# Three rearrangements in a two-block transformer kernel: modulation insertions joined, the end of a recurrent block taken by chunks, and stick-breaking attention begun inside the stage that makes its values

## The reference, cut to what matters

```python
mod = (s_lat @ w_ada[l] + b_ada[l])[:, None, :]
mod_c = s_ctx @ w_ada[l] + b_ada[l]
...
u = dwconv1d(h @ w_up, dw, dw_b)
a, g = jnp.split(u, 2, axis=-1)
return (jax.nn.silu(g) * a) @ w_down
```

```python
z = jnp.einsum('bhqd,bhkd->bhqk', q[:, :, t0:L], k[:, :, :L])
log_keep = jnp.where(mask, jax.nn.log_sigmoid(-z), 0.0)
later = lax.cumsum(log_keep, axis=3, reverse=True) - log_keep
w = jnp.where(mask, jnp.exp(jax.nn.log_sigmoid(z) + later), 0.0)
outs.append(jnp.einsum('bhqk,bhkd->bhqd', w, v[:, :, :L]))
...
a = jnp.exp(log_a)
b = jnp.sqrt(-jnp.expm1(2.0 * log_a)) * (i * xc).astype(jnp.float32)
_, hs = lax.associative_scan(_lin_rec_combine, (a, b), axis=1)
y = jax.nn.gelu(gate) * hs.astype(h.dtype)
return y @ w_out
```

## Time and profile before

| | |
|---|---|
| median of 3 runs | 2291.49 us (2282.19 to 2295.35) |
| the profiled execution's own time | 2294.72 us |
| its span, first to last instruction | 2293.1 us, mean granted clock 0.989 |
| PE busy | 2210.9 us, 96% |
| DVE busy | 1819.1 us, 79% |
| ACT busy | 1297.8 us, 57% |
| transfers | 499.80 MB, mean 218 GB/s |
| matmuls of three-way products, start to start | 0.12 us |

### The profile page before, as it was taken

One profiled execution on the slowest core, in us unless ns is written; L12 is line 12 of the kernel. 1 busy time (PEld: TensorE's weight loads), 2 busy tenths in 40 slices (PEclk: granted clock), 3 DMA queues, 4 the chain that ended last, 5 costly groups with the idle time before them and its releaser, 6 DMA issues.

```text
span 2293.1 us, 49211 instructions
## 1 busy us (share of the span) xinstructions
PE 2210.9 (96%) x18000; PEld 2122.8 (93%) x18000; DVE 1819.1 (79%) x3186; ACT 1297.8 (57%) x2102; POOL 119.8 (5%) x231
## 2 busy tenths in 40 slices
PE   6999999999999999999999999989999999979998
PEld 4898899998899999889999999987999999979998
DVE  4886867799699988978998878767877877878655
ACT  3465755536776553576665644646544644686443
POOL 0100000000000100000000011010000001000000
PEclk8999999999999999999999999999999999999999
DMA  9746666765358865534778678662778677636654
GB/s 356 277 138 203 230 236 204 257 202 162 123 184 273 271 222 199 176 117 170 256 268 278 225 274 269 213 237 88 247 270 267 236 274 264 235 106 192 219 171 132
DMA packets 150550, 499.80 MB, mean 218 GB/s; under 512 B 17408, under 2 KB 21632, under 8 KB 148864
## 3 DMA queue, kind: packets, MB, share of 16 engines
q1 hardware_dynamic: 113504, 374.01, 47.4%
q0 software_dynamic: 32544, 119.55, 16.5%
q10 hardware_dynamic: 4352, 4.20, 0.6%
HBM read 496.65 MB, written 1.05 MB: 217 GB/s over the span
## 4 chain that ended last, share of the span: by engine, by line
PE 70%; DVE 14%; ACT 6%; DMA 5%; issue 4%; ACTq 0%; DVEq 0%; SPq 0%; POOLq 0%; POOL 0%
PE bank_pair L1922 21%; PE bank_pair L1924 20%; PE bank_pair L1923 20%; DVE w_lo L1173 4%; DMA modraw<-in_w_mod 3%; ACT w_hi L636 2%; DVE arena L1460 2%; PE bank_pair L2045 2%; PE ps_o L1935 1%; DVE small L1540 1%; DVE modraw L1201 1%; ACT arena L875 1%; DVE arena L1329 1%; DMA raw<-in_w_down 1%; PE ps_o L2354 1%
## 5 line engine op out<-in xcount | busy, mean ns | idle before, releaser
L1173 DVE TENSOR_TENSOR w_lo<-raw,w_hi 128x1024 fp32r<-128x1024 f32 (+2 forms) x748 | 821.1, 1113 | 189.1 <-ACT w_hi L636 185.6
L636 ACT ACTIVATE w_hi<-raw 128x1024 fp32r<-128x1024 f32 (+2 forms) x748 | 713.4, 967 | 391.9 <-PE bank_pair L1924 257.6
L1922 PE MATMUL bank_pair<-h_hi,w_hi 128*128 128x256 f32 x2928 | 839.0, 287 | 10.5 <-DVE arena L1737 4.2
L1923 PE MATMUL bank_pair<-h_lo,w_hi 128*128 128x256 f32 x2928 | 829.5, 283 | 0.0
L1924 PE MATMUL bank_pair<-h_hi,w_lo 128*128 128x256 f32 x2928 | 829.4, 283 | 0.0
L1922 PE MATMUL bank_pair<-e_both,w_hi 128*128 128x256 f32 (+1 forms) x2064 | 593.7, 288 | 18.7 <-DVE e_both L1857 10.0
L1922 PEld LDWEIGHTS bank_pair<-h_hi,w_hi 128*128 128x128 f32 x2928 | 561.5, 192 | 31.2 <-issue 24.2
L1923 PE MATMUL bank_pair<-e_both,w_hi 128*128 128x256 f32 (+1 forms) x2064 | 585.6, 284 | 0.0
L1924 PE MATMUL bank_pair<-e_both,w_lo 128*128 128x256 f32 (+1 forms) x2064 | 585.5, 284 | 0.0
L1923 PEld LDWEIGHTS bank_pair<-h_lo,w_hi 128*128 128x128 f32 x2928 | 562.0, 192 | 0.3
L1924 PEld LDWEIGHTS bank_pair<-h_hi,w_lo 128*128 128x128 f32 x2928 | 561.8, 192 | 0.0
(11 more groups left out here) (250 smaller groups left out, 2103.9 us busy)
## 6 DMA issues: line engine op xcount, KB each, us to landing
modraw<-in_w_mod POOLq DMA_DIRECT2D x216, 512.0 KB, 5.0
raw<-in_w_gu SPq DMA_DIRECT2D x176, 512.0 KB, 4.6
raw<-in_w_up SPq DMA_DIRECT2D x132, 512.0 KB, 5.1
raw<-in_w_gate SPq DMA_DIRECT2D x48, 512.0 KB, 3.9
raw<-in_w_dn SPq DMA_DIRECT2D x64, 384.0 KB, 4.6
raw<-in_w_dn SPq DMA_DIRECT2D x64, 320.0 KB, 3.5
raw<-in_w_down SPq DMA_DIRECT2D x48, 384.0 KB, 5.1
raw<-in_w_down SPq DMA_DIRECT2D x48, 320.0 KB, 4.8
```

The lines of the kernel that those rows point to most:

```text
L636: nc.scalar.activation(w_hi[:, p, HALF * f:HALF * f + w], raw[:, p, HALF * f:HALF * f + w], ACT.Copy)\
L1173: nc.vector.tensor_tensor(w_lo[:, p, at], raw[:, p, HALF * f:HALF * f + w], w_hi[:, p, at].bitcast(F32), ALU.subtract).then_inc(lo_ready, 1)
L1922: nc.tensor.matmul(out, l[0], r[0], start=start, stop=False)
L1923: nc.tensor.matmul(out, l[0], r[1], start=False, stop=False)
```

## The change

Three edits in different stages.

1. **Up stage of the context.** Both halves of a modulation and the turn of the one before are now inserted together, between the halves of the slab with p=1 (`whole`). The slab with p=0 has no insertion. The stage's last turn and its sum move from the stage's end into the first slab of the next stage (`last_turn`).
2. **Stick-breaking.** The helpers `st_scores`, `st_terms` and so on replace the inline code. Inside value slab k, between its halves, PE makes scores(k) and, from k=2 on, sums(k-2). DVE has softplus(k-1), mask(k) and add(k-2) there ahead of the modulation products, ACT terms(k-1), and in the last slab weights(0). `do_stick` starts at i=3 (`ST_AHEAD`). Scores go to the banks `ps_t`, sums to `ps_o`, outputs to bank pair 1. The seven unread matmuls are gone. The last two modulation products of the value stage move from iteration 1 to iteration 8. ACT's table load for Exp and Ln stands in the first value slab, before in the last.
3. **End of the recurrence.** The products by the root move ahead of the splits of slab 8, so both stand before the first scan. Low parts 0 to 5 are made before the second scan. In the first body PE takes chunks 0 to 5 of slab 0, chunks 0 to 4 of slab 1, then 6 to 9 of slab 0 and the rest of slab 1, with eight unread matmuls ahead and three between (`LRU_WARM`).

```diff
+        def whole(s):
+            return s.kind == "upa"
...
+        def last_turn(s, b, p):
+            q = s.prev
+            if q is not None and q.turn_end and isinstance(b, int) and (b, p) == (0, 0):
+                return q.m0 + q.mods * q.bodies - 1
+            return None
...
# ACT, value stage
-                        if last and p == 1 and s.arg["heads"] == SB_H:
-                            act.preload_act_table_set("natural_log_exp_and_others")
+                        if s.arg["heads"] == SB_H:
+                            if 2 * b + p == 0:
+                                act.preload_act_table_set("natural_log_exp_and_others")
+                            else:
+                                st_terms(2 * b + p - 1)
+                            if 2 * b + p >= 3:
+                                st_weights(2 * b + p - 3)
...
# DVE, value stage
                         if s.arg["heads"] == SB_H:
-                            lambda_part(4 + 2 * b + p)
+                            k = 2 * b + p
+                            if k >= 1:
+                                st_softplus(k - 1)
+                            st_mask(k)
+                            if k >= 2:
+                                st_add(k - 2)
+                            lambda_part(4 + k)
...
# DVE, do_stick
+                for i in range(ST_AHEAD, SB_P + 3):
+                    if ST_AHEAD < i <= SB_P:
+                        st_softplus(i - 1)
                     if i + 1 < SB_P:
+                        st_mask(i + 1)
+                    st_low(i - 3)
+                    if i <= SB_P:
+                        st_add(i - 1)
+                    if i == SB_P:
                         mods(sv, sv.bodies - 1, 1, False, True)
...
# DVE, recurrence
                         if j == 7:
                             lru_square(1)
+                            for f in range(2):
+                                lru_input(f)
                         if j == 8:
                             lru_scan(0)
...
             def do_lru(n):
                 lru_outs(0)
+                lru_lows(0)
                 lru_scan(1)
-                lru_lows(0)
                 lru_outs(1)
                 lru_lows(1)
...
# PE
             def mods(s, b, p):
-                if s.m0 >= N_PE or not s.mods:
+                if last_turn(s, b, p) is not None:
+                    mod_turns(last_turn(s, b, p))
+                if s.m0 >= N_PE or not s.mods or whole(s) and p == 0:
                     return
...
+            def lout_first(s, p):
+                n, early = RC // 2, LRU_PARTS[0].stop
+                if p == 0:
+                    free_banks(s, 0, 1, True)
+                    pe.wait_ge(lru_gates, RC)
+                    keep_warm(LRU_WARM[0])
+                    pe.wait_ge(lo_ready, 2 * s.l0 + 1)
+                    for k in range(n):
+                        ins = lout_chunk(s, 0, k)
+                    ins.then_inc(half_done, 1)
+                    pe.wait_ge(lo_ready, 2 * s.l0 + 2)
+                    for k in range(n, early):
+                        lout_chunk(s, 0, k)
+                    pe.wait_ge(lo_ready, 2 * s.l0 + 3)
+                    for k in range(n):
+                        lout_chunk(s, 1, k)
+                    keep_warm(LRU_WARM[1])
+                    for k in range(early, RC):
+                        ins = lout_chunk(s, 0, k)
+                    ins.then_inc(half_done, 1)
+                else:
+                    pe.wait_ge(lo_ready, 2 * s.l0 + 4)
+                    lout_chunk(s, 1, n).then_inc(half_done, 1)
+                    for k in range(n + 1, RC):
+                        ins = lout_chunk(s, 1, k)
+                    ins.then_inc(half_done, 1)
...
# PE, value stage
                             half(s, b, p, 0, is_first)
                             mods(s, b, p)
+                            if s.kind == "v" and s.arg["heads"] == SB_H:
+                                st_scores(2 * b + p)
+                                if 2 * b + p >= 2:
+                                    st_sums(2 * b + p - 2)
```

More of the change, by code:

```diff
@@ L1909, in _ @@
                 kinds[s.kind](s) if what == "slabs" else others[what](s)
-                if what == "slabs" and s.turn_end:
-                    mod_sums(s.m0 + s.mods * s.bodies - 1)
         @block.tensor
@@ L2021, in _ @@
                     plain = s["plain"] + DC
+            stick = next(s for what, s in plan if what == "stick")
             def b_is_one(b):
@@ L2197, in out_first, with keep_warm, lout_chunk @@
                             ins.then_inc(half_done, 1)
+            def keep_warm(n):
+                for _ in range(n):
+                    nc.tensor.matmul(ps_t[:, 0, 0:T], ones, table("cos"), start=True, stop=True)
+            def lout_chunk(s, p, k):
+                pe.wait_ge(lru_lo, k + 1)
+                f, n = k // (RC // 2), k % (RC // 2)
+                c = HALF * f + P * n
+                return mm3(pb[p][:, 0, 0:T], (w_hi[:, p, c:c + P], w_lo[:, p, c:c + P]),
+                           (e_hi[:, k, :], e_lo[:, k, :]), k == 0, k == RC - 1)
+            def lout_first(s, p):
[24 more added lines that the diff above has]
+                    ins.then_inc(half_done, 1)
             def open_pair(i):
@@ L2227, in body @@
                             merge_first(s)
+                        elif s is after_lru and is_first:
+                            lout_first(s, p)
                         elif s.kind == "out" and is_first and p == 0:
@@ L2365, in do_gate @@
                     merge_heads(s.nxt, c)
-            def keep_warm(n):
-                for _ in range(n):
-                    nc.tensor.matmul(ps_t[:, 0, 0:T], ones, table("cos"), start=True, stop=True)
             def do_stick(n):
                 so = next(s for what, s in plan if what == "slabs" and s.kind == "out" and s.arg["kind"] == "b")
-                pe.wait_ge(tab_in, 16)
-                pe.wait_ge(q_copied, n["had"]["q"])
-                pe.wait_ge(v_copied, n["had"]["v"] - 1)
-                for i in range(-1, SB_P + 2):
+                pe.wait_ge(v_copied, n["had"]["v"])
@@ L2379, in do_stick @@
+                for i in range(ST_AHEAD, SB_P + 2):
+                    if i == ST_AHEAD:
+                        st_out(0)
                     if i + 1 < SB_P:
[L2380 to L2388 removed]
@@ L2405, in do_stick @@
[L2405 to L2417 removed]
+                        st_scores(i + 1)
```

173 lines of the change are left out of this document (88 added, 85 removed).

## The result

The changed kernel takes 2272.09 us (median of 7 runs, 2270.9 to 2272.97), the kernel before 2291.49 us (7 runs, 2282.19 to 2295.35). The ratio is 0.9923, 95% interval 0.9912 to 0.9934. The profiled execution took 2272.4 us with a span of 2270.7 us; that of before had a span of 2293.1 us. The forecast was 2271 us.

A forecast was written before the change was run, and what follows sets the result against it. PE, busy for 96% of the span, was taken to bound the kernel. Gains of 5.0 + 11.6 + 4.1 = 20.7 us give 2274.0 us from the profiled 2294.72, 2270.8 from the median 2291.49; forecast 2271 us, range 2260 to 2283.

The forecast's parts named there:

- Edit 1, 5.0 us forecast: Up stage: joined insertions save 0.32 us in each of 11 bodies, 3.5 us, and an idle turn's 1.5 us goes.
- so the 1.5 us go: Up stage, second body: the turn, moved behind ACT's copy of its row, no longer stands idle for 1.52 us.
- The last turn only changes place: End of the up stage: the final turn moves without gain or loss, about 0.2 us of matmuls.
- joining saves nothing: Rival, up stage: slabs without insertions end waiting for DVE's taps, gain 0 instead of 5, 2275.8 us; chance 0.08.
- Edit 2, 11.6 us forecast: Value stage and stick-breaking: softplus(3) starts at about 1542.6 instead of 1554.17, then the same 3.9 us a pair.
- The schedule worked out: Value stage and stick-breaking: order laid out by hand from 1505.3, the first value matmul, to softplus(3) at about 1542.6.
- Only one of the six products that I follow waited over 1 us: Value stage: held against the slower case, late loads holding PE up, 2302 us; chance 0.04.
- The reason in one sentence: Stick-breaking before: mask(0) behind four modulation products came 5 us after its scores; the ring filled with nothing else on PE.
- The two products at iteration 8: Stick-breaking: 2.3 us of DVE work makes low part 6 1.1 us later, hidden by PE's output projection; cost nothing.
- The clock: Rival, stick-breaking and recurrence's end: stretches at 1.2 GHz, about 5 us less gain, 2275.8 us; chance 0.10.
- Edit 3, 4.1 us forecast: Recurrence's end: PE through slab 1 4.7 us earlier, less 0.6 us waiting for a bank; bounds 2.5 to 5.
- the fourth slab waits 0.6 us for its bank: Last projection: DVE only 2.6 us earlier with its updates, so PE loses 0.6 us of the 4.7 us gained.

The follow-up runs named there:

- halves_apart: The changed kernel with the two halves of the modulation products apart as before and the turn with the second half; 2277.73 us.
- mask_first: The kernel before with the last body's two modulation products of the first value section put behind mask(0) and mask(1); 2290.29 us, ratio 1.0003.
- products_early: The changed kernel with the last two modulation products at iteration 3 instead of 8; 2277.76 us.
- softplus_first: The changed kernel with softplus(k+1) ahead of add(k) on DVE in the stick-breaking loop; 2277.66 us.
- no_warm: The changed kernel without the unread matmuls at the recurrence's end; 2273.79 us, ratio 0.992.
- turn_third: The changed kernel with the turn left in the third slab of each body pair, the products joined; 2272.62 us.

## Why the prediction was right, step by step

- **Edit 1, 5.0 us forecast; 4.4 in the pair of profiles, 4.7 on the mean.** Joining was priced at 0.32 us a body and measured at 0.33 (13.25 to 12.92), 3.6 us for 11. The step that was mis-sized is the idle turn, "so the 1.5 us go": 0.56 us came back at 260.50, where the turn now waits for the sum of the turn before on DVE. At the stage's end one wait took another's place: 1.15 us at 384.63, for 1.07 us before `down`'s second slab. "The last turn only changes place" is true in its sum only. The step's reason was also half: the c=0 products waited for the same copy (`halves_apart`). That joining saves nothing is excluded.
- **Edit 2, 11.6 us forecast; 11.4 in the pair of profiles, 10.9 on the mean.** The schedule worked out held. With the 6.1 us between the two starts taken off, softplus(3) was forecast for 1536.5 and came at 1536.56, add(1) to end at 1531.2 and came to 1531.7. The loads, copied at 8.4 us, were kinder in section 1 (it ended 0.8 us early) and less kind in section 2 (0.5 us late), and neither told, as the DVE work behind waits for ACT from 1532.70 on. "Only one of the six products that I follow waited over 1 us" misreads the trace: the one at 1529.65 waited 1.28 us. "The reason in one sentence" is borne out only in its second half, "the ring was filled with nothing else on PE". For the first, the products ahead of mask(0), `mask_first` gives 1.3 us of 10.9 and leaves the rest open, and the unread matmuls that held up the third pair's scores aren't in it.
- **The two products at iteration 8** were put at nothing and cost nothing; elsewhere they cost 2.9 us.
- **The clock** was left up in the sum, and was 1.00. The waits that took it down in other runs were those of `products_early` or `softplus_first`.
- **Edit 3, 4.1 us forecast; 4.7 in the pair, 4.4 on the mean.** The first chunk was forecast for 2055.8, which is 2038.2 with the shift of 17.6 us taken off, and came at 2038.18. The term that failed is "the fourth slab waits 0.6 us for its bank": from 2045.91 to the end of the projection PE doesn't wait. DVE's first update is 2.8 us earlier (2046.46 against 2066.93, less the shift), as forecast about 2.6, and its last one 4.1 us (2067.25 against 2089.02): DVE had idle time in each slab, so it ran behind PE and caught up. That the unread matmuls "cost nothing" holds; what they bring is 0.2 us to the end of slab 1, nothing clear of noise in the stretch. PE's idle time there was forecast as "some 3 us in three pieces" and was 1.74 us in four.
- **The sum.** 20.7 forecast, 20.5 in the pair of profiles, 20.0 by means over the kernels, and 17.6 by the ratio (15.1 to 20.2), which the forecast gain lies just above. That the time came out 1.1 us from 2271 is in part luck: what no edit touches varied by 4.8 us from one profile to another, and the kernel before by 13 us from run to run.

## What to carry to other kernels

When a chain over three engines follows a stage in which the bounding engine is full, begin the chain inside that stage: here its links lengthened the value stage by 7.2 us and shortened stick-breaking by 18.7 us. Before an instruction is moved in one engine's order, follow the whole round through every engine's queue, as the order of ACT turned what looked like a shorter loop on DVE into one of 5.49 us. An idle time at an instruction belongs to everything that waits for the same thing: moving the turn alone gained nothing.

## What the hardware showed unexpectedly

- Between fp32 three-way matmuls of 128x256, doing eight narrow fp32 products (128x32 weights) in two runs of four instead of one costs 0.32 us (`halves_apart` 13.24 us a body, changed kernel 12.92); a break with the turn's two matmuls alone costs nothing beyond them (`turn_third`, 12.92 us).
- PE at the 1.2 GHz level (0.21 us a matmul instead of 0.12, for 28 matmuls, some 2.6 us in all) cost 0.2 us at the end of slab 1 in `no_warm`, where PE would otherwise have waited for DVE.
